# Input stage of a hybrid decoder block: layer norm of the meta tokens and the low-rank rests on other engines, and another order of turned pieces

## The chip, the cores and the metric

The kernel runs on one core of one Trainium2 chip. The metric is the device time of one execution in microseconds (us). Engines: TensorE (PE), VectorE (DVE), ScalarE (ACT), GpSimd (POOL) and SyncE (SP, which here only issues transfers).

## The reference

16 learned meta tokens are put ahead of 256 tokens, all of width 2048, and go through a layer norm, whose output feeds every projection of the block.

```python
def layer_norm(x, g, b):
    mu = jnp.mean(xf, axis=-1, keepdims=True)
    var = jnp.mean(jnp.square(xf - mu), axis=-1, keepdims=True)
    return ((xf - mu) * lax.rsqrt(var + LN_EPS) * g + b).astype(x.dtype)

h = layer_norm(jnp.concatenate([meta, x], axis=1), ln_in_g, ln_in_b)
p = h @ w_in[l]     # r, k, v (2048 columns each), low-rank wl, al, gl (96 + 96 + 256), pool (1024), gates (4096)
...                 # rwkv7 time mixing and causal pooling, merged by gates, output product, layer norm
h = layer_norm(DN_ALPHA * h + peer_ffn(h, ...), ln2_g[l], ln2_b[l])   # 8 x 16 experts per token, gathered rows
return h[:, N_META:]
```

## The kernel before

The program is a row of stages, each a block that all engines enter together and leave together: the input stage (`front_stage`), the time mixing, the merge, the output product, and the routing with the experts, whose rows are gathered from memory. The change is in `front_stage` alone.

**What the stage computes.** The tokens lie as rows: `xm` (16 meta tokens, in the memory of `x_turned1`), and `k.h[:, 0]` and `k.h[:, 1]` (128 tokens each, 2048 wide). Each tile is measured (`measure`: four `bn_stats`, aggregate, plus eps, reciprocal), its deviation is the `Sqrt` of ScalarE (`root`), and `centre` subtracts the mean and scales, in place. TensorE turns the tiles by transposes, 128 columns at a time (`turn`), into three PSUM tiles used in rotation; ScalarE evacuates with gamma and beta as scale and bias into `x_turned`; VectorE splits the result into a rounded part and its rest (`rounded`), which together are hT, the stationary input's partner in every product. Each product is made of three matmuls (high by high, high by rest, rest by high: `product`).

**Pieces.** A piece is four of the sixteen 128-column blocks of one token tile; `PIECES` lists (tile, quarter) in order. The meta tokens are turned apart, as 16 narrow transposes, and evacuated by VectorE.

**Low-rank products.** The 448 low-rank columns of `w_in` come in four quarters of the contraction. ScalarE rounds a quarter (`round_lora`, 128 x 1792), VectorE makes its rest (`rest_lora`), and TensorE runs the products of a quarter for four column tiles (`project`, 12 matmuls each) once `quarter_ready(g)` has seen 1 + 2 (g + 1) increments of `s_hT` and g + 1 of `s_wsplit`. Quarter 0 has the turning of pieces 4 to 7 woven into it. Quarters 2 and 3 run column tile by column tile. Then come 48 matmuls of the first half-tiles of r.

**Queues and order.** Every engine runs its list in order, written out by hand:

- SP loads x, the low-rank weights, three w_half, the constants; then it waits for `s_hT` to reach 8 and 9 and loads gamma and beta as wide rows (1 MB each) over `x_turned0` and `x_turned1`; then three more w_half, each behind a `rest_half`.
- ACT: root(0), copy of gamma and beta vectors, root(1), `round_lora(0)`, then the eight pieces, with root(2) ahead of piece 1 and `round_lora` 1 and 2 ahead of pieces (0, 2) and (0, 3), `round_lora(3)`, three `round_half`, and the low-rank outputs.
- DVE: measure meta, measure x0, centre meta, centre x0, measure x1, meta's evacuation, centre x1, split of meta, then `rounded` of the pieces with the four `rest_lora` between them, small vectors, three `rest_half`, and at the end, behind the wide rows, four passes over h (2048 wide) with the four low-rank mixes between them.
- POOL: two memsets and small loads, then nothing.

Of the kernel before, what the change touches and what calls it, by code (L numbers as in the profile page):

```python
# [9 lines left out]
ALU = mybir.AluOpType  # L10
# [3 lines left out]
P = 128  # L14
D = 2048
# [185 lines left out]
def front_stage(k, w):  # L201

    nc = k.nc
    with ExitStack() as ctx:
# [5 lines left out]
        stats, mv, rs = sb("ln_stats", [P, 3, 4, 6]), sb("ln_mean_var", [P, 3, 2]), sb("ln_rstd", [P, 3, 2])  # L210
# [13 lines left out]
        tiles = [(xm, META), (k.h[:, 0, :], P), (k.h[:, 1, :], P)]  # L224
        ORDER4 = (2, 3, 0, 1)
        PIECES = ((0, 0), (0, 1), (1, 0), (1, 1), (0, 2), (1, 2), (0, 3), (1, 3))
        QK, HK = KT // 4, KT // 2
        block = ctx.enter_context(nc.Block())

# [17 lines left out]
        @block.gpsimd  # L247
        def _(pool):
            mu = w["mu_shift"][0, 0:3 * D].rearrange("(r c) -> r c", c=P)
            nc.gpsimd.memset(raw[:], 0.0).then_inc(s_zero, 1)  # L250
            nc.gpsimd.memset(k.mu_lora[:], 0.0).then_inc(s_zero, 1)
            pool.wait_ge(s_zero, 2)
            rows = [mu] + [w[n][0].rearrange("(r c) -> r c", c=P) for n in ("w0", "a0", "k_k", "k_a")]
            rows += [w["r_k"][0].rearrange("(r two) c -> r (two c)", two=2)]
            rows += [w[n][0].rearrange("(r c) -> r c", c=P) for n in ("gn_g", "gn_b")]
            rows += [w["b_gate"][0].rearrange("b (r c) -> (b r) c", c=P), w["pool_scale"][0].rearrange("(r c) -> r c", c=P)]
            at = 0
            for r in rows:
                done = 0
                while done < r.shape[0]:  # L260
                    n = min(r.shape[0] - done, P - at % P)
                    pool.dma_start(raw[at % P:at % P + n, at // P, :], r[done:done + n, :]).then_inc(s_raw, 16)
                    done, at = done + n, at + n
            for i, (c0, n) in enumerate(k.lora_tiles):
                pool.dma_start(k.mu_lora[0:n, i:i + 1], w["mu_shift"][0, c0:c0 + n].rearrange("(n a) -> n a", a=1)).then_inc(s_raw, 16)

        n_dma = 10 + len(k.lora_tiles)

        @block.tensor
        def _(pe):  # L270
# [3 lines left out]
            pe.wait_ge(s_h, 1)  # L274
            for kt in range(KT):
                mm = nc.tensor.transpose(tp[0][:, kt * META:(kt + 1) * META], xm[:, kt * P:(kt + 1) * P], ident[0:META, 0:META])
            mm.then_inc(s_turn, 1)
            def turn(n):
                t, q = PIECES[n]
                pe.wait_ge(s_h, t + 2)  # L280
                if n == 2:
                    pe.wait_ge(s_meta_ev, 1)
                if n > 2:
                    pe.wait_ge(s_ev, n - 2)
                for j in range(4):
                    mm = nc.tensor.transpose(tp[(n + 1) % 3][:, j * P:(j + 1) * P], k.h[:, t, (4 * q + j) * P:(4 * q + j + 1) * P], ident)
                mm.then_inc(s_turn, 1)

            for n in range(4):
                turn(n)  # L290
            pe.wait_ge(s_raw, 16 * n_dma)
            pe.wait_ge(s_gb, 1)
            nc.tensor.transpose(pv[:, 0:P], raw[:, 0, :], ident)
            nc.tensor.transpose(pv[:, P:2 * P], raw[:, 1, :], ident).then_inc(s_pv, 1)

            def project(i, g):
                c0, n = k.lora_tiles[i]
                for kt in range(QK * g, QK * g + QK):
                    mm = product(nc, pp[i][0:n, :], [x[:, kt, c0 - LORA0:c0 - LORA0 + n] for x in (lhigh, lrest)],
                                 (k.hT_high[:, kt, :], k.hT[:, kt, :]), kt == 0, kt == KT - 1)  # L300
                return mm
# [12 lines left out]
            for i in ORDER4:
                for g in range(2, 4):
                    if i == ORDER4[0]:
                        quarter_ready(g)
                    mm = project(i, g)
                mm.then_inc(s_mm, 1)
            for kt in range(KT):  # L320
                g, kh = divmod(kt, HK)
                if kh == 0:
                    pe.wait_ge(k.s_split, g + 1)
                mm = product(nc, k.project[0][:, 0:T], (k.w_high[g][:, kh, :], k.w_rest[g][:, kh, :]),
                             (k.hT_high[:, kt, :], k.hT[:, kt, :]), kt == 0, kt == KT - 1)
                if kh == HK - 1:
                    mm.then_inc(k.s_used, 1)

        @block.scalar
        def _(act):  # L330
# [5 lines left out]
            def root(i):  # L336
                n = tiles[i][1]
                act.wait_ge(s_var, i + 1)
                nc.scalar.activation(rs[0:n, i, 1:2], rs[0:n, i, 0:1], ACT.Sqrt).then_inc(s_rstd, 1)

            root(0)
            act.wait_ge(s_gb_turn, 1)
            nc.scalar.copy(gb[:], pv[:, 256:256 + 2 * KT]).then_inc(s_gb, 1)
            def round_lora(g):
                act.wait_ge(s_w[g], 16)
                nc.scalar.copy(lhigh[:, QK * g:QK * g + QK, :].bitcast(F32R), lraw[:, QK * g:QK * g + QK, :]).then_inc(s_wround, 1)

            root(1)
            act.wait_ge(s_gb, 1)
            round_lora(0)  # L350
            for n, (t, q) in enumerate(PIECES):
                if n == 1:
                    root(2)
                if (t, q) in ((0, 2), (0, 3)):
                    round_lora(q - 1)
                act.wait_ge(s_turn, n + 2)
# [31 lines left out]
        def _(dve):  # L388
            v, d = nc.vector, nc.vector.drain

            def measure(i):
                x, n = tiles[i]
                for j in range(4):
                    v.bn_stats(stats[0:n, i, j, :], x[:, 512 * j:512 * (j + 1)])
                d()
                v.bn_aggr(mv[0:n, i, :], stats[0:n, i, :, :])
                d()
                v.tensor_scalar(rs[0:n, i, 0:1], mv[0:n, i, 1:2], LN_EPS, None, ALU.add)
                d()
                v.reciprocal(rs[0:n, i, 0:1], rs[0:n, i, 0:1]).then_inc(s_var, 1)  # L400

            def centre(i):
                x, n = tiles[i]
                dve.wait_ge(s_rstd, i + 1)
                v.tensor_scalar(x, x, mv[0:n, i, 0:1], rs[0:n, i, 1:2], ALU.subtract, ALU.mult).then_inc(s_h, 1)

            def rounded(n):
                t, q = PIECES[n]
# [6 lines left out]
            dve.wait_ge(s_meta, 16)  # L415
# [18 lines left out]
            def rest_lora(g):  # L434
                dve.wait_ge(s_wround, g + 1)
                rest_bits(v, lrest[:, QK * g:QK * g + QK, :], lraw[:, QK * g:QK * g + QK, :], lhigh[:, QK * g:QK * g + QK, :]).then_inc(s_wsplit, 1)
# [12 lines left out]
            rest_lora(3)  # L449
            dve.wait_ge(s_pv, 1)  # L450
            v.tensor_copy(k.vec[:, 0:8, :], pv[:, 0:P].rearrange("p (v r) -> p v r", r=16))
            v.tensor_copy(k.vec[:, 8:NRAW, :], pv[:, P:P + 64].rearrange("p (v r) -> p v r", r=16))
# [18 lines left out]
                v.tensor_tensor(k.h[:, t, :], k.h[:, t, :], g, op)  # L471

            dve.wait_ge(s_wide, 32)
            dve.wait_ge(s_turn, 1 + 4 * TT)
            residual(gam, ALU.mult, 0)
            mix(0)
            residual(gam, ALU.mult, 1)
# [1506 lines left out]
```

## Time and profile before

| | us |
|---|---|
| median of 3 runs | 2472.67 (2469.45 to 2474.23) |
| span of the profiled execution, its own time | 2469.5 |
| input stage, up to the first matmul of the next stage | 58.9 |
| TensorE / VectorE / ScalarE busy in the first 58.9 us | 40.61 / 45.44 / 27.05 |
| GpSimd busy in the same | 7.88 |
| TensorE / VectorE busy in the span | 2193.7 / 1533.5 |

The profile is of one execution. Lines Lnnn are those of the kernel's file. Matmuls are pipelined, so the shown duration of one is longer than the spacing between two. A helper's line (L182, `rest_bits`, and L197, `product`) stands for all its callers; the tiles' names tell them apart.

### The profile page before, as it was taken

The page shows a single profiled execution, that of the slowest core. Times are in us where ns is not written, and L with a number is a line of the kernel's source. Part 1 is how long each engine was busy: PE and PEld are TensorE (multiplying, and loading weights), DVE is VectorE, ACT ScalarE, POOL GpSimd, SP SyncE. Part 2 cuts the span into 40 slices and gives each one's busy share as a digit, 9 for nine tenths or more (in the row PEclk, how much of TensorE's full clock was granted, in tenths as well). Part 3 has the DMA queues.
Part 4 walks back from the last instruction along what each step waited for, and adds up shares of the span by engine and source line. Part 5 has one row for each costly group of instructions (what it writes and reads, how often), then busy time and mean ns, then how long its engine had stood idle before and what let it go on. Part 6 is the DMA issues. An engine that isn't in the chain of part 4 may idle for free.

```text
span 2469.5 us, 39419 instructions
## 1 busy us (share of the span) xinstructions
PE 2193.7 (89%) x16183; PEld 1536.9 (62%) x16183; DVE 1533.5 (62%) x2579; ACT 727.0 (29%) x1383; POOL 664.8 (27%) x541
## 2 busy tenths in 40 slices
PE   7999999999999999999989888988787787777776
PEld 6899999999989999988644444533332232222222
DVE  7777777787764554456855776677445544444445
ACT  4555555555434444342211111111111000000000
POOL 1000000000000000002555545555545445444442
PEclk9999999999999999999999999999999999999999
DMA  5433333333347666484999999999999999999997
GB/s 198 137 94 86 100 88 89 97 90 86 97 120 224 184 187 182 139 303 181 404 420 423 423 426 427 427 427 428 427 427 427 426 427 427 427 427 427 427 427 290
DMA packets 346278, 708.29 MB, mean 287 GB/s; under 512 B 13834, under 2 KB 270434, under 8 KB 279778
## 3 DMA queue, kind: packets, MB, share of 16 engines
q0 software_dynamic: 74176, 537.01, 51.7%
q1 hardware_dynamic: 271684, 168.55, 23.3%
q8 instruction: 129, 2.11, 0.3%
q14 instruction: 49, 0.40, 0.0%
q10 hardware_dynamic: 240, 0.22, 0.0%
HBM read 703.63 MB, written 2.10 MB: 286 GB/s over the span
## 4 chain that ended last, share of the span: by engine, by line
DMA 33%; PE 15%; DVE 2%; issue 2%; POOL 1%; DVEq 0%; ACT 0%; POOLq 0%; ACTq 0%
DMA down_rows<-in_v_table,experts 25%; PE bank L1695 11%; DMA up_rows<-in_u_table,experts 8%; PE bank L1611 2%; POOL down_rows L1599 1%; DVE up_rows L1811 0%; PE bank L1638 0%; PE bank L1653 0%; PE bank L1659 0%; ACT diagonal L1755 0%; DVE one_hot L1251 0%; DVE expert_sides L1257 0%; PE bank L1621 0%; PE bank L1665 0%; DVE side_index L1230 0%
## 5 line engine op out<-in xcount | busy, mean ns | idle before, releaser
L1695 PE MATMUL bank<-down_rows,diagonal 128*128 128x512 f32 x2032 | 947.7, 611 | 210.7 <-DMA down_rows<-in_v_table,experts 173.1
L1811 DVE CUSTOM_DVE_ANT_0 up_rows<-up_rows,h 128x2048 f32<-128x2048 f32 x256 | 585.2, 2292 | 523.2 <-DMA up_rows<-in_u_table,experts 523.2
L1695 PEld LDWEIGHTS bank<-down_rows,diagonal 128*128 128x128 f32 x2032 | 375.2, 193 | 741.9 <-issue 385.7
L1593 POOL DMA_INDIRECT up_rows<-in_u_table,experts x256 | 286.0, 1117 | 1207.2 <-POOLq L1269 1091.4
L1599 POOL DMA_INDIRECT down_rows<-in_v_table,experts x256 | 370.3, 1446 | 523.5 <-PE bank L1695 510.5
L182 DVE TENSOR_TENSOR w_half_rest<-w_half,w_half_high 128x1024 fp32r<-128x1024 f32 x224 | 273.0, 1221 | 180.8 <-ACT w_half_high L161 178.9
L197 PE MATMUL project<-hT_high,w_half_high 128*128 128x272 f32 (+1 forms) x1152 | 353.5, 307 | 1.6 <-DVE r L909 1.3
L197 PE MATMUL project<-hT_high,w_half_rest 128*128 128x272 f32 (+1 forms) x1152 | 330.6, 287 | 0.0
L197 PE MATMUL project<-hT,w_half_high 128*128 128x272 f32 (+1 forms) x1152 | 330.0, 287 | 0.0
L161 ACT CAST w_half_high<-w_half 128x1024 fp32r<-128x1024 f32 x224 | 234.7, 1051 | 191.3 <-PE merge_ps L197 122.0
L197 PEld LDWEIGHTS project<-hT_high,w_half_high 128*128 128x128 f32 x1152 | 216.9, 188 | 11.3 <-DVE r L909 1.5
L1774 ACT ACTIVATE dots<-dots 128x4 f32<-128x4 f32 x64 | 13.3, 207 | 713.9 <-DVE dots L1811 713.9
L197 PEld LDWEIGHTS project<-hT,w_half_high 128*128 128x128 f32 x1152 | 217.0, 188 | 2.4
L197 PEld LDWEIGHTS project<-hT_high,w_half_rest 128*128 128x128 f32 x1152 | 216.9, 188 | 0.0
L1755 ACT ACTIVATE diagonal<-constants_kept,weights 128x128 f32<-128x128 f32 x256 | 82.3, 394 | 280.0 <-DVE weights L1818 280.0
L1611 PE MATMUL bank<-h1T,query_w 128*128 128x256 f32 x256 | 65.1, 388 | 10.2 <-ACT queryT L1720 10.2
L197 PE MATMUL merge_ps<-yaT_high,w_half_high 128*128 128x256 f32 x256 | 72.7, 284 | 1.4 <-PEq L514 1.4
L1611 PEld LDWEIGHTS bank<-h1T,query_w 128*128 128x128 f32 x256 | 49.5, 194 | 38.2 <-issue 33.8
L197 PE MATMUL merge_ps<-yaT_high,w_half_rest 128*128 128x256 f32 x256 | 72.4, 283 | 0.0
L197 PE MATMUL merge_ps<-yaT_rest,w_half_high 128*128 128x256 f32 x256 | 72.4, 283 | 0.0
L197 PE MATMUL merge_ps<-hT,w_half_high 128*128 128x256 f32 x256 | 72.1, 282 | 0.0
L197 PE MATMUL merge_ps<-hT_high,w_half_rest 128*128 128x256 f32 x256 | 72.0, 281 | 0.0
(338 smaller groups left out, 3013.2 us busy)
## 6 DMA issues: line engine op xcount, KB each, us to landing
w_half<-in_w_in SPq DMA_DIRECT2D x176, 512.0 KB, 4.0
w_half<-in_w_branch_a SPq DMA_DIRECT2D x32, 512.0 KB, 3.9
out_w<-in_w_out SPq DMA_DIRECT2D x16, 1024.0 KB, 5.3
query_w<-in_w_q_peer SPq DMA_DIRECT2D x10, 1024.0 KB, 19.7
w_half<-in_w_branch_b SPq DMA_DIRECT2D x16, 512.0 KB, 3.8
out_w<-in_w_q_peer SPq DMA_DIRECT2D x6, 1024.0 KB, 29.5
up_rows<-in_u_table,experts POOLq DMA_INDIRECT x256, 21.1
down_rows<-in_v_table,experts POOLq DMA_INDIRECT x256, 20.5
```

Of the source, the lines that this page charges most:

```text
L161: self.nc.scalar.copy(self.w_high[g % 3][:].bitcast(F32R), self.w_raw[g % 3][:]).then_inc(self.s_rounded, 1)
L182: return eng.tensor_tensor(low.bitcast(F32R), x, high, ALU.subtract)
L197: mm = nc.tensor.matmul(out, a.bitcast(F32R), b.bitcast(F32R), start=start and n == 0, stop=stop and n == 2)
L1593: pool.indirect_dma_start(ur[n % RU][:], None, w["u_table"][0], bass.IndirectOffsetOnAxis(ap=k.idx[:, t, h, j:j + 1], axis=0)).then_inc(s_ ...
L1599: pool.indirect_dma_start(vr[n % RV][:], None, w["v_table"][0], bass.IndirectOffsetOnAxis(ap=k.idx[:, t, h, j:j + 1], axis=0)).then_inc(s_ ...
L1611: mm = nc.tensor.matmul(pq[i][:, 0:SEQ], k.query_part(h, i, kt), k.h1T[:, kt, :], start=(kt == 0), stop=(kt == KT - 1))
L1695: mm = nc.tensor.matmul(acc[t][c][:], dg[n % RD][:], vr[n % RV][:, quarter(c)], start=(n == 0), stop=(n == last(t, c)), skip_group_check=True)
L1755: nc.scalar.activation(dg[n % RD][:], ident, ACT.Copy, scale=weights[:, n:n + 1]).then_inc(s_diag, 1)
L1774: nc.scalar.activation(x, x, ACT.Gelu).then_inc(s_gelu, 1)
L1811: v.tensor_tensor_reduce(ur[n % RU][:], ur[n % RU][:], k.h[:, n // (HEADS * TOPK), :], 1.0, 0.0, ALU.mult, ALU.add, dots[:, n:n + 1]).then ...
```

## The change

- Meta's sums move to ScalarE: a `Copy` and a `Square` with an accumulated output, and a small step for minus the mean. VectorE only adds eps and takes the reciprocal of 16 values, ScalarE takes the root, GpSimd centres.
- The four rests of the low-rank weights move from VectorE to GpSimd.
- `PIECES` alternates between the token tiles from the first on. TensorE turns piece 0 before the meta tokens, then pieces 1 and 2; piece 3 now comes behind the first 12 low-rank matmuls.
- Each token tile is centred in two instructions, the first 512 columns and the other 1536. For the second tile these lie on either side of the splits of pieces 0 and 1 and of meta.

```diff
-        PIECES = ((0, 0), (0, 1), (1, 0), (1, 1), (0, 2), (1, 2), (0, 3), (1, 3))
+        PIECES = ((0, 0), (1, 0), (0, 1), (1, 1), (0, 2), (1, 2), (0, 3), (1, 3))
+        scrap, sums = turned[0][0:META].rearrange("p k t -> p (k t)"), sb("meta_sums", [META, 4])
@@ gpsimd
+            pool.wait_ge(s_meta_dev, 1)
+            nc.gpsimd.tensor_scalar(xm, xm, minus_mean, deviation, ALU.add, ALU.mult).then_inc(s_meta_h, 1)
+            for g in range(4):
+                pool.wait_ge(s_wround, g + 1)
+                own = slice(QK * g, QK * g + QK)
+                rest_bits(nc.gpsimd, lrest[:, own, :], lraw[:, own, :], lhigh[:, own, :]).then_inc(s_wsplit, 1)
@@ tensor
-                pe.wait_ge(s_h, t + 2)
+                pe.wait_ge(s_h, t * 2 + (1 if q == 0 else 2))
...
-            for n in range(4):
-                turn(n)
+            turn(0)
+            turn_meta()
+            turn(1)
+            turn(2)
...
+                    if g == 0 and n == 0:
+                        turn(3)
@@ scalar
-            root(0)
+            def meta_sums():
+                act.wait_ge(s_meta, 16)
+                nc.scalar.activation(scrap, xm, ACT.Copy, accum_out=total).then_inc(s_meta_sum, 1)
+                act.wait_ge(s_meta_sum, 1)
+                nc.scalar.activation(minus_mean, total, ACT.Copy, scale=-1.0 / D).then_inc(s_meta_sum, 1)
+                act.wait_ge(s_meta_sum, 2)
+                nc.scalar.activation(scrap, xm, ACT.Square, bias=minus_mean, accum_out=squares).then_inc(s_meta_sq, 1)
+            meta_sums()
+            act.wait_ge(s_meta_var, 1)
+            nc.scalar.activation(deviation, squares, ACT.Sqrt).then_inc(s_meta_dev, 1)
             act.wait_ge(s_gb_turn, 1)
             nc.scalar.copy(gb[:], pv[:, 256:256 + 2 * KT]).then_inc(s_gb, 1)
...
-            root(1)
+            root(0)
             act.wait_ge(s_gb, 1)
             round_lora(0)
             for n, (t, q) in enumerate(PIECES):
                 if n == 1:
-                    root(2)
+                    root(1)
@@ vector
+            FIRST, OTHERS = slice(0, 512), slice(512, D)
             measure(0)
-            dve.wait_ge(s_x[0], 16)
-            measure(1)
-            centre(0)
-            centre(1)
-            dve.wait_ge(s_x[1], 16)
-            measure(2)
-            dve.wait_ge(s_gb, 1)
-            dve.wait_ge(s_turn, 1)
+            dve.wait_ge(s_meta_sq, 1)
+            v.tensor_scalar(squares, squares, 1.0 / D, LN_EPS, ALU.mult, ALU.add)
+            d()
+            v.reciprocal(squares, squares).then_inc(s_meta_var, 1)
+            centre(0, FIRST)
+            centre(0, OTHERS)
+            measure(1)
+            dve.wait_ge(s_meta_turn, 1)
...
-            centre(2)
-            d()
+            centre(1, FIRST)
+            rounded(0)
             v.tensor_copy(k.hT_high[:, :, 0:META].bitcast(F32R), meta_turned[:])
...
-            rounded(0)
-            rest_lora(0)
-            rounded(2)
             rounded(1)
-            rounded(3)
-            rest_lora(1)
-            rounded(4)
-            rounded(5)
-            rest_lora(2)
-            rounded(6)
-            rounded(7)
-            rest_lora(3)
+            centre(1, OTHERS)
+            for n in range(2, len(PIECES)):
+                rounded(n)
```

## Rows read from the trace of the kernel before

**Rows 1.** Top of the page.
```profile
span 2469.5 us, 39419 instructions
```

**Rows 2.** Timeline of PE, 0 to 62 us: start, duration, what [idle before it].
```profile
24.43 0.60 PE L197 MATMUL lora_project<-hT_high,lora_weights_high 128*128 128x272 f32 x1 [2.63 <-DVE hT L182]
...
28.45 0.43 PE L197 MATMUL lora_project<-hT_high,lora_weights_rest 128*128 128x272 f32 x1
28.68 0.38 PE L197 MATMUL lora_project<-hT_high,lora_weights_high 128*128 128x272 f32 x1
...
34.19 0.37 PE L197 MATMUL lora_project<-hT_high,lora_weights_high 128*128 128x272 f32 x1
...
40.30 0.29 PE L197 MATMUL lora_project<-hT_high,lora_weights_high 128*128 128x272 f32 x1
...
58.90 0.36 PE L197 MATMUL project<-hT_high,w_half_high 128*128 128x272 f32 x1 [0.33 <-PEq L204]
```

**Rows 3.** Timeline of DVE, 0 to 60 us.
```profile
8.29 2.44 DVE L394 BATCH_NORM_STATS2 ln_stats<-h 128x6 f32<-128x512 f32 x4
...
11.37 0.16 DVE L400 RECIPROCAL ln_rstd<-ln_rstd 128x1 f32<-128x1 f32 x1
...
12.69 1.33 DVE L405 TENSOR_SCALAR h<-h,ln_mean_var,ln_rstd 128x2048 f32<-128x2048 f32 x1
...
17.66 0.42 DVE L428 TENSOR_TENSOR meta_turned<-meta_turned,ln_in_vectors 128x256 f32<-128x256 f32 x1
...
37.73 0.42 DVE L411 CAST hT_high<-x_turned 128x512 fp32r<-128x512 f32 x1
38.23 0.69 DVE L182 TENSOR_TENSOR hT<-x_turned,hT_high 128x512 fp32r<-128x512 f32 x1
39.09 2.03 DVE L182 TENSOR_TENSOR lora_weights_rest<-lora_weights,lora_weights_high 128x1792 fp32r<-128x1792 f32 x1 [0.16 <-ACT lora_weights_high L346]
...
46.80 2.29 DVE L471 TENSOR_TENSOR h<-h,x_turned 128x2048 f32<-128x2048 f32 x1 [1.28 <-DMA x_turned<-in_ln_in_b]
...
57.02 0.49 DVE L467 SCALAR_TENSOR_TENSOR lora<-lora_project,mu_lora,lora 96x271 f32<-96x271 f32 x1
```

**Rows 4.** DMA issues in 0 to 64 us: size, time to landing.
```profile
x_turned<-in_ln_in_b SPq DMA_DIRECT2D x1, 1024.0 KB, 7.8
```

**Rows 5.** DMA issues in 0 to 0.9 us.
```profile
h<-in_x SPq DMA_DIRECT2D x1, 1024.0 KB, 6.2
```

**Rows 6.** Timeline of ACT, 0 to 60 us.
```profile
11.67 0.21 ACT L339 ACTIVATE ln_rstd<-ln_rstd 128x1 f32<-128x1 f32 x1
12.96 1.69 ACT L346 CAST lora_weights_high<-lora_weights 128x1792 fp32r<-128x1792 f32 x1 [1.08 <-DMA lora_weights<-in_w_in]
...
31.55 1.52 ACT L359 ACTIVATE x_turned<-project,ln_in_vectors 128x128 f32<-128x128 f32 x4
32.93 1.72 ACT L346 CAST lora_weights_high<-lora_weights 128x1792 fp32r<-128x1792 f32 x1
34.52 1.55 ACT L359 ACTIVATE x_turned<-project,ln_in_vectors 128x128 f32<-128x128 f32 x4
```

**Rows 7.** Groups by form, POOL.
```profile
L250 POOL MEMSET raw_vectors<- 128x256 f32 x1 | 0.3, 312 | 0.3 <-POOLq L1976 0.3
...
L251 POOL MEMSET mu_lora<- 128x4 f32 x1 | 0.1, 102 | 0.0
```

**Rows 8.** Timeline of POOL, 1155 to 1260 us, expert stage.
```profile
1231.15 1.91 POOL L1593 DMA_INDIRECT up_rows<-in_u_table,experts  x1 [0.31 <-issue]
1233.37 2.77 POOL L1599 DMA_INDIRECT down_rows<-in_v_table,experts  x1 [0.30 <-issue]
1236.44 0.94 POOL L1593 DMA_INDIRECT up_rows<-in_u_table,experts  x1 [0.30 <-issue]
```

**Rows 9.** Timeline of DVE, same stretch.
```profile
1232.65 0.41 DVE L1807 TENSOR_SCALAR gates<-gates,gate_rsum 128x16 f32<-128x16 f32 x1
1233.03 2.29 DVE L1811 CUSTOM_DVE_ANT_0 up_rows<-up_rows,h 128x2048 f32<-128x2048 f32 x1
```

More of the change, by code:

```diff
@@ L209, in front_stage @@
         raw, gb_raw, gb = sb("raw_vectors", [P, 2, P]), sb("ln_in_rows", [2 * KT, P]), sb("ln_in_vectors", [P, 2 * KT])
-        stats, mv, rs = sb("ln_stats", [P, 3, 4, 6]), sb("ln_mean_var", [P, 3, 2]), sb("ln_rstd", [P, 3, 2])
+        stats, mv, rs = sb("ln_stats", [P, TT, 4, 6]), sb("ln_mean_var", [P, TT, 2]), sb("ln_rstd", [P, TT, 2])
         xm = turned[1][0:META].rearrange("p k t -> p (k t)")
@@ L223, in front_stage @@
         ident = k.kept[:, C_ID:C_ID + P]
-        tiles = [(xm, META), (k.h[:, 0, :], P), (k.h[:, 1, :], P)]
         ORDER4 = (2, 3, 0, 1)
-        PIECES = ((0, 0), (0, 1), (1, 0), (1, 1), (0, 2), (1, 2), (0, 3), (1, 3))
+        PIECES = ((0, 0), (1, 0), (0, 1), (1, 1), (0, 2), (1, 2), (0, 3), (1, 3))
+        scrap, sums = turned[0][0:META].rearrange("p k t -> p (k t)"), sb("meta_sums", [META, 4])
+        total, minus_mean, squares, deviation = (sums[:, i:i + 1] for i in range(4))
+        s_meta_sum, s_meta_sq, s_meta_var, s_meta_dev, s_meta_h, s_meta_turn = (k.sem(f"in_meta_{n}") for n in ("sum", "squares", "var", "deviation", "h", "turned"))
         QK, HK = KT // 4, KT // 2
@@ L273, in _, with turn_meta @@
             nc.tensor.transpose(pv[:, 256:256 + 2 * KT], gb_raw[:], ident[0:2 * KT, 0:2 * KT]).then_inc(s_gb_turn, 1)
[L274 to L277, printed above, removed]
+            def turn_meta():
+                pe.wait_ge(s_meta_h, 1)
+                for kt in range(KT):
+                    mm = nc.tensor.transpose(tp[0][:, kt * META:(kt + 1) * META], xm[:, kt * P:(kt + 1) * P], ident[0:META, 0:META])
+                mm.then_inc(s_meta_turn, 1)
             def turn(n):
                 t, q = PIECES[n]
-                pe.wait_ge(s_h, t + 2)
+                pe.wait_ge(s_h, t * 2 + (1 if q == 0 else 2))
                 if n == 2:
@@ L334, in _, with root @@
                 act.dma_start(gb_raw[n * KT:(n + 1) * KT, :], w[g].rearrange("(r c) -> r c", c=P)).then_inc(s_gb_raw, 16)
[L336 to L339, printed above, removed]
-            root(0)
+            def root(t):
+                act.wait_ge(s_var, t + 1)
+                nc.scalar.activation(rs[:, t, 1:2], rs[:, t, 0:1], ACT.Sqrt).then_inc(s_rstd, 1)
+            def meta_sums():
[8 more added lines that the diff above has]
+            nc.scalar.activation(deviation, squares, ACT.Sqrt).then_inc(s_meta_dev, 1)
             act.wait_ge(s_gb_turn, 1)
@@ L352, in _ @@
                 if n == 1:
-                    root(2)
+                    root(1)
                 if (t, q) in ((0, 2), (0, 3)):
                     round_lora(q - 1)
-                act.wait_ge(s_turn, n + 2)
+                act.wait_ge(s_turn, n + 1)
                 for j in range(4):
@@ L389, in _, with measure, centre @@
             v, d = nc.vector, nc.vector.drain
-            def measure(i):
-                x, n = tiles[i]
+            def measure(t):
+                dve.wait_ge(s_x[t], 16)
                 for j in range(4):
-                    v.bn_stats(stats[0:n, i, j, :], x[:, 512 * j:512 * (j + 1)])
+                    v.bn_stats(stats[:, t, j, :], k.h[:, t, 512 * j:512 * (j + 1)])
                 d()
-                v.bn_aggr(mv[0:n, i, :], stats[0:n, i, :, :])
+                v.bn_aggr(mv[:, t, :], stats[:, t, :, :])
                 d()
-                v.tensor_scalar(rs[0:n, i, 0:1], mv[0:n, i, 1:2], LN_EPS, None, ALU.add)
+                v.tensor_scalar(rs[:, t, 0:1], mv[:, t, 1:2], LN_EPS, None, ALU.add)
                 d()
[L400 to L405, printed above, removed]
+                v.reciprocal(rs[:, t, 0:1], rs[:, t, 0:1]).then_inc(s_var, 1)
+            def centre(t, own):
+                x = k.h[:, t, own]
+                dve.wait_ge(s_rstd, t + 1)
+                v.tensor_scalar(x, x, mv[:, t, 0:1], rs[:, t, 1:2], ALU.subtract, ALU.mult).then_inc(s_h, 1)
             def rounded(n):
@@ L413, in rounded @@
                 rest_bits(v, k.hT[:, own, at], turned[t][:, own, :], k.hT_high[:, own, at]).then_inc(s_hT, 1)
-            dve.wait_ge(s_meta, 16)
+            FIRST, OTHERS = slice(0, 512), slice(512, D)
             measure(0)
-            dve.wait_ge(s_x[0], 16)
-            measure(1)
-            centre(0)
-            centre(1)
-            dve.wait_ge(s_x[1], 16)
-            measure(2)
-            dve.wait_ge(s_gb, 1)
-            dve.wait_ge(s_turn, 1)
+            dve.wait_ge(s_meta_sq, 1)
[4 more added lines that the diff above has]
+            centre(0, OTHERS)
+            measure(1)
+            dve.wait_ge(s_meta_turn, 1)
             wide = lambda c: gb[:, c * KT:(c + 1) * KT].rearrange("p (k a) -> p k a", a=1).to_broadcast((P, KT, META))
@@ L433, in _ @@
             rest_bits(v, k.hT[:, :, 0:META], meta_turned[:], k.hT_high[:, :, 0:META]).then_inc(s_hT, 1)
-            def rest_lora(g):
-                dve.wait_ge(s_wround, g + 1)
-                rest_bits(v, lrest[:, QK * g:QK * g + QK, :], lraw[:, QK * g:QK * g + QK, :], lhigh[:, QK * g:QK * g + QK, :]).then_inc(s_wsplit, 1)
-            rounded(0)
-            rest_lora(0)
-            rounded(2)
-            rounded(1)
-            rounded(3)
-            rest_lora(1)
-            rounded(4)
-            rounded(5)
-            rest_lora(2)
-            rounded(6)
-            rounded(7)
-            rest_lora(3)
+            rounded(1)
+            centre(1, OTHERS)
+            for n in range(2, len(PIECES)):
+                rounded(n)
             dve.wait_ge(s_pv, 1)
@@ L473, in _ @@
             dve.wait_ge(s_wide, 32)
-            dve.wait_ge(s_turn, 1 + 4 * TT)
+            dve.wait_ge(s_turn, 4 * TT)
             residual(gam, ALU.mult, 0)
```

## The prediction

> **What bounds the kernel now.** I read the page first for the span, 2469.5 us [rows 1]; the launch adds nothing to it that the times show, since the shown runs' median is 2472.67 and their lowest 2469.45. The sum below is made against the 2469.5 of the profiled execution and its difference is then added to 2472.67. The change lies wholly in the input stage, so I read the timelines of that stage, engine by engine. TensorE is the one that sets its end: it starts the low-rank products at 24.43, released by a hT from VectorE, and runs without a hole to 58.57, since the first matmul of the next stage stands at 58.90 with 0.33 of idle ahead of it [rows 2]. Inside lie three gates: quarter 1 begins at 34.19, quarter 2 at 40.30, quarter 3 twelve matmuls later, 40.30 + 12 x 0.125 = 41.8, and 16.8 us follow that. Early matmuls come 0.23 us apart (28.45 to 28.68), later ones (6.1 us for the 48 of quarter 1) about 0.127. The engine had idled 2.63 before 24.43, and the spacing halves 4.2 us after it; that is the step from its 1.2 to its 2.4 GHz level [rows 2].
>
> VectorE is close behind. It waits until 46.80 for the second wide row (ln_in_b), then needs 10.7 us for four multiplications and additions of h and the four mixes, and ends at 57.51 [rows 3], only 1.06 before TensorE. That transfer is issued when the ninth hT is counted, at 38.23 + 0.69 = 38.92 [rows 3], and lands 7.8 us later [rows 4]. So the stage has two ends: TensorE's products, and ninth hT + 18.6 us.
>
> **The change part by part.** *Meta off VectorE.* Measuring a tile takes 11.53 - 8.29 = 3.24 there, and centring it 1.33 (rows of x; the same lengths hold for 16 partitions) [rows 3]. The second instruction group started at 8.29, so the meta tokens were there at about 5.1; x's first tile is there at 0.75 + 6.2 = 6.95 [rows 5]. So x0's measure now ends at 10.2, 1.3 earlier. ScalarE's two passes over 2048 elements cost at most 1.72 x 2048 / 1792 = 2.0 each [rows 6], 5.1 to 9.4 with the small one, hidden under x0's measure. VectorE's two small steps end about 10.6, ScalarE's root 10.85.
>
> But root(0) stands behind the copy of the gamma and beta vectors, which put the root of x0 at 11.67 to 11.88 before [rows 6], and nothing there moves. x0 cannot be centred before 11.95.
>
> *Meta's centring on GpSimd.* No row of before shows GpSimd reading an operand and writing a result. Its nearest rows are the memsets: 312 ns for 256 elements, 102 for 4 [rows 7], or 0.83 ns per element for one access. One access for 2048 elements is 1.8 us, two in turn 3.5. I take 2.2, nearer the lower end because the one read and the one write can overlap: 10.9 to 13.1. Three and a half would put the first half-stage 1.3 later at most.
>
> *Low-rank rests on GpSimd.* VectorE does one of 1792 elements in 2.03 [rows 3]; four are removed from it, 8.1 us. GpSimd's floor is the same 2.0; two accesses in turn are 3.1, three (two reads, one write) 4.6. I take 3.8, between the two memset multiples, and keep 2.0 and 4.6. The Trainium skill, GPSIMD Engine Reference, section 3.1, gives 4497 ns for a two-input operation of 2048 elements; as an estimate that is 3.9 for 1792, and the sum would be 0.4 dearer by it. No run here shows it yet.
>
> *Can the two engines work side by side?* In the expert stage a GpSimd gather issue takes 0.94 alone (1236.44), but the one that began at 1233.37 under a two-input VectorE instruction (1233.03 to 1235.32) took 2.77 and ended 0.82 after that one's end; and VectorE's scaling of 16 elements at 1232.65 took 0.41 and ended at 1233.06, the instant at which the GpSimd issue of 1231.15 ended [rows 8, 9]. Each waits for the other, whole instruction by whole instruction. I take this for the rests too, since hT's casts and rests work on the same memory; that they do not wait is the second rival. The Trainium skill, SBUF — State Buffer, section Who interferes with whom, says this as a rule: the pair of ports is locked for a whole instruction, by GpSimd, by VectorE's fast copies and scalings, and for reads by its two-input operations. By that rule the sum is the 5.6 worked out below; without it, the second rival's -1.0. These two rows agree with it.
>
> *The front half with this.* x0's centring waits for GpSimd: first quarter 13.1 to 13.5, the rest to 14.5; x1 measured by 17.8. Rest 0 on GpSimd runs from 14.65, when the first rounding ends [rows 6], to 18.45. Meta's multiply ends at 18.2, its addition (0.42 [rows 3]) has two inputs and waits: 18.45 to 18.85. Centring x1's first quarter to 19.3, four transposes to 20.4, four evacuations (1.4) to 21.85, rounding and rest of the piece (0.42 and 0.69, start to end 1.15 [rows 3]) to 23.1. TensorE starts about 23.15, a gain of 1.3.
>
> *Quarters 0 and 1.* Before, from start to quarter 1 was 9.75. One piece more is now turned inside, four transposes, at the fast spacing at most 4 x 0.127 = 0.5: 10.25, so 33.4. That turn(3) also moves ScalarE: its evacuation comes only after 12 slow matmuls, 23.15 + 2.7 + 0.9, and ends at 28.0. Behind it in ScalarE's order stand rounding 1 (1.6 start to start, evacuations 1.4 [rows 6]): to 29.6, pieces 4 and 5 to 32.4, rounding 2 to 34.0, pieces 6 and 7 to 36.8, rounding 3 to 38.4, only a little ahead of where it ended before (VectorE's last rest, at 39.09, had waited for it [rows 3]). So ScalarE's chain gives nothing back, and rest 1 is 29.6 to 33.4, just in time for 33.4.
>
> *Quarters 2 and 3.* VectorE's rounding of piece 4 is ready at 31.0 but waits for rest 1: 33.4 to 34.6. Rest 2, ready at 34.0, then holds to 38.4. VectorE casts piece 5 to 38.85, rest 3 slips into the gap ahead of its rest and holds to 42.65. Behind it come the rest of piece 5 (43.35), piece 6 (44.5), piece 7 (45.6). TensorE needs piece 5 at 33.4 + 6.1 = 39.5 and gets it at 43.35; quarter 3 opens at 45.6 in place of 41.8, so it ends at 45.6 + 16.8 = 62.4. The ninth hT comes 45.6 - 38.92 = 6.7 late. SP's queue holds the w_half loads behind the wide rows; the next stage needs them only some 4 us into it, and they have that. VectorE ends 57.51 + 6.7 = 64.2, the next stage starts 0.33 later at 64.5: **5.6 us later than 58.90**.
>
> Later stages begin at a barrier behind this one and pass a shift on whole: 2469.5 + 5.6 = 2475.1 for a profile, and 2472.67 + 5.6 = 2478.3 for the median.
>
> With GpSimd's rest at 4.6 the ninth hT falls at 30.4 + 3 x 4.6 + 4.6 = 48.8: +8.8. At 3.1 the turns interleave better and it is 43.25: +3.3. At 2.0 nothing is late and the earlier start remains: -1.0.
>
> **Rivals.** *VectorE keeps the memory between its cast and its rest, or the GpSimd rest costs about 3.1.* Then pieces 4 and 5 go together to 35.7, rest 2 to 39.5, pieces 6 and 7 to 41.8, rest 3 to 45.6. The wide rows are 2.9 late, but TensorE waits for rest 3 at 45.6 and the next stage begins at 62.7: +3.8, median 2476.5; the cheaper rest gives +3.3. For it: nothing in rows 8 and 9 has exactly a cast with its drain. Against it: rest 3 is last in either order, so the sum hardly falls below 3.
>
> *The engines run side by side* (other side: no slower). Then x0 is centred at 11.95, TensorE starts at 21.75, quarter 1 at 32.0, ScalarE's last rounding ends at 37.0, rest 3 at 40.8, where TensorE arrives at 39.6. It ends at 40.8 + 16.8 = 57.6: -1.0, 2471.7. The ninth hT is 2.4 early, so VectorE does not decide. With a rest of 3.1 it is -1.7. It decides from a rest under 4.8 on, and needs that rows 8 and 9 mean something of the gather alone. Against it stand both their directions.
>
> *Dearer.* The stall of nearly 4 us before quarter 2 is longer than the 2.63 behind which TensorE ran at its lower level: a second such stretch costs 4.2 / 2 = 2.1, TensorE ends at 64.5 and the next stage begins at 64.8, 0.3 more. Also the w_half loads are released only 2.2 us after the last wide row instead of 4.3, and can slow its landing by up to 2. Together +7.9: 2480.6.
>
> *A gain that can be measured* would need 4.9 us. Even the earliest start and a free rest give 2.
>
> **How the numbers follow.** Within 0.2%, 4.9 us, is about what a measurement of this kernel cannot tell from no change. The likeliest, GpSimd in the gaps with 3.6 to 4.6 per rest, gets 0.45 (+5 to +8.8, 2477.7 to 2481.5 for itself); the smaller loss of 3.3 to 3.8, 0.36; side by side 0.11; the dearer one 0.05; a gain of over 4.9 by something not seen, 0.03. So slower 0.45 + 0.05 = 0.50, same 0.36 + 0.11 = 0.47, faster 0.03. The time is that of the likeliest, 2478.3. The range goes from 2471.5 (side by side) to 2482 (a rest of 4.6 and some loss of landing).
>
> **What the profile after would show.** Right: first low-rank matmul near 23.2; GpSimd rests of 3.8; hT casts of pieces 4 to 6 starting at the end of a GpSimd rest, or stretched; TensorE idle before quarter 2 or 3; wide rows issued near 45; next stage at 64.5. Wrong: hT casts of 0.42 in the midst of a GpSimd rest (side by side), or rests near 2 us, or the wide row landing before 48. The forecast fails most easily by who gets the memory first, and by the length of one GpSimd rest, each 0.1 us of which counts 0.4.

## The result, and the profile after

The changed kernel takes 2477.57 us (median of 13 runs, 2475.35 to 2479.27) against 2471.95 for the one before (13 runs): ratio 1.0027, 95% interval 1.002 to 1.0034, so 0.27% or 6.6 us slower (the two medians by themselves lie 5.6 apart). The forecast was 2478.3, 5.6 more than before.

The page of the profiled execution has the span:

```profile
span 2476.0 us, 39420 instructions
```

That is 6.5 more than [rows 1]. TensorE's timeline (start, duration, what, idle before it) shows where it comes from:

```profile
23.53 0.59 PE L197 MATMUL lora_project<-hT_high,lora_weights_high 128*128 128x272 f32 x1 [1.54 <-DVE hT L182]
...
34.85 0.36 PE L197 MATMUL lora_project<-hT_high,lora_weights_high 128*128 128x272 f32 x1 [0.76 <-POOL lora_weights_rest L182]
...
44.62 0.40 PE L197 MATMUL lora_project<-hT_high,lora_weights_high 128*128 128x272 f32 x1 [3.50 <-DVE hT L182]
...
65.40 0.36 PE L197 MATMUL project<-hT_high,w_half_high 128*128 128x272 f32 x1 [0.89 <-PEq L204]
```

The next stage begins at 65.40 where it was 58.90 [rows 2]: 6.50 later, as much as the whole difference of the two spans. TensorE starts its products 0.9 earlier, waits 0.76 for GpSimd's rest 1 before quarter 1 and 3.50 for VectorE's hT before quarter 2, and has no hole after that. GpSimd's timeline:

```profile
11.15 2.04 POOL L269 TENSOR_SCALAR x_turned<-x_turned,meta_sums 16x2048 f32<-16x2048 f32 x1 [2.50 <-ACT meta_sums L364]
14.82 3.97 POOL L182 TENSOR_TENSOR lora_weights_rest<-lora_weights,lora_weights_high 128x1792 fp32r<-128x1792 f32 x1 [1.63 <-ACT lora_weights_high L369]
30.66 4.04 POOL L182 TENSOR_TENSOR lora_weights_rest<-lora_weights,lora_weights_high 128x1792 fp32r<-128x1792 f32 x1 [11.87 <-ACT lora_weights_high L369]
35.04 4.07 POOL L182 TENSOR_TENSOR lora_weights_rest<-lora_weights,lora_weights_high 128x1792 fp32r<-128x1792 f32 x1 [0.33 <-ACT lora_weights_high L369]
39.42 4.09 POOL L182 TENSOR_TENSOR lora_weights_rest<-lora_weights,lora_weights_high 128x1792 fp32r<-128x1792 f32 x1 [0.32 <-ACT lora_weights_high L369]
```

A rest takes 3.97 to 4.09, twice VectorE's 2.03 [rows 3]. VectorE's timeline beside it:

```profile
11.92 2.54 DVE L428 TENSOR_SCALAR h<-h,ln_mean_var,ln_rstd 128x512 f32<-128x512 f32 x2 [1.34 <-ACT ln_rstd L352]
...
18.06 1.02 DVE L451 TENSOR_TENSOR meta_turned<-meta_turned,ln_in_vectors 128x256 f32<-128x256 f32 x1
...
32.02 2.96 DVE L434 CAST hT_high<-x_turned 128x512 fp32r<-128x512 f32 x1 [1.79 <-ACT x_turned L382]
35.06 4.59 DVE L182 TENSOR_TENSOR hT<-x_turned,hT_high 128x512 fp32r<-128x512 f32 x1
39.58 4.22 DVE L434 CAST hT_high<-x_turned 128x512 fp32r<-128x512 f32 x1
...
46.07 0.69 DVE L182 TENSOR_TENSOR hT<-x_turned,hT_high 128x512 fp32r<-128x512 f32 x1
...
54.36 2.29 DVE L482 TENSOR_TENSOR h<-h,x_turned 128x2048 f32<-128x2048 f32 x1 [3.19 <-DMA x_turned<-in_ln_in_b]
...
64.58 0.49 DVE L478 SCALAR_TENSOR_TENSOR lora<-lora_project,mu_lora,lora 96x271 f32<-96x271 f32 x1
```

Read the two together. The cast of piece 4 (0.42 before) begins at 32.02 inside rest 1, lasts 2.96 and ends 0.28 after it. The rest of the same piece (0.69 before) is issued at 35.06, 0.02 after rest 2, lasts 4.59 and ends 0.54 after it. The cast of piece 5 is issued at 39.58, inside rest 3, and lasts 4.22. These three have become 11.77 us where they were 1.53. The last rest of a piece, the ninth hT, ends at 46.76, where [rows 3] have 38.92. The second wide row lands at 54.36, and VectorE ends at 65.07, 7.56 later than before. Its transfer was no dearer (time to landing, 7.8 in [rows 4]):

```profile
x_turned<-in_ln_in_b SPq DMA_DIRECT2D x1, 1024.0 KB, 7.5
```

ScalarE's timeline: the rounding for rest 1 begins at 28.89, because piece 3 is turned inside the products, and rounding 3 ends at 39.34, nearly where it ended before. The table load at 9.55 is new; the root of meta waits for it.

```profile
9.55 1.28 ACT L364 ACT_TABLE_LOAD   x1
10.84 0.20 ACT L364 ACTIVATE meta_sums<-meta_sums 16x1 f32<-16x1 f32 x1
...
28.89 1.70 ACT L369 CAST lora_weights_high<-lora_weights 128x1792 fp32r<-128x1792 f32 x1
...
37.54 1.80 ACT L369 CAST lora_weights_high<-lora_weights 128x1792 fp32r<-128x1792 f32 x1
```

The window after the hole shows what else it cost. Its columns are the length of the window, the busy time of TensorE, its weight loads, VectorE, ScalarE and GpSimd (with instructions in brackets), then the granted TensorE clock (PEclk), the DMA share and GB/s:

```profile
45.00:49.00 4.00, 4.00 (x22) 4.00 (x21) 3.83 (x13) 0.00 (x0) 0.00 (x0) 0.57 0.63 221
```

Between 45 and 49 the granted clock is 0.57, mostly its lower level of 1.2 GHz, after 3.50 idle; these 4 us hold 22 matmuls, and the same window of the kernel before holds 34. From 49 on the clock reads 1.00 again.

### The profile page after: what moved, and what is told of

The parts are those of the page before. It is cut to its first block, busy times and chain, and to the rows that moved or that the text cites. A ratio compares the mean times of both kernels' runs of the same rounds, so it can differ in the third digit from the quotient of the medians.

```text
span 2476.0 us, 39420 instructions
## 1 busy us (share of the span) xinstructions
PE 2194.6 (89%) x16183; PEld 1537.8 (62%) x16183; DVE 1533.4 (62%) x2571; ACT 730.7 (30%) x1389; POOL 682.6 (28%) x546
## 4 chain that ended last, share of the span: by engine, by line
DMA 33%; PE 15%; DVE 2%; issue 2%; POOL 1%; DVEq 1%; ACT 0%; POOLq 0%; ACTq 0%
DMA down_rows<-in_v_table,experts 25%; PE bank L1706 12%; DMA up_rows<-in_u_table,experts 8%; PE bank L1622 2%; POOL down_rows L1610 1%; DVE up_rows L1822 0%; PE bank L1649 0%; PE bank L1664 0%; PE bank L1670 0%; ACT diagonal L1766 0%; DVE one_hot L1262 0%; PE bank L1638 0%; DVE expert_sides L1268 0%; PE bank L1632 0%; PE bank L1676 0%
```

## The experiments

Theory: GpSimd's rests and VectorE's casts and rests exclude each other for whole instructions, and this delays hT. Rivals: the new order of pieces costs the time; or GpSimd's rests are merely slow and TensorE waits for them.

**All four rests back on VectorE**, the rest of the change kept.

```diff
-            for g in range(4):      # gpsimd
-                pool.wait_ge(s_wround, g + 1)
-                ...
+            rest_lora(0)            # vector, ahead of rounded(1)
             rounded(1)
             centre(1, OTHERS)
+            ...                     # rest_lora(1), (2), (3) behind pieces 3, 5, 7
```

> The changed kernel with the four low-rank rests back on VectorE (rest 0 ahead of piece 1, the others as before); all else of the change stays. Theory (GpSimd and VectorE exclude each other instruction by instruction, and that makes hT and so the wide rows late): no cast or rest of VectorE longer than 0.7 us (rests 2.03), TensorE starts its low-rank products about 24.5 (rest 0 stands ahead), no hole before quarter 2, ninth hT about 39.7, next stage about 59.4, whole kernel 0 to +1 us against the one before. Rival (the new order of pieces and the turning of piece 3 inside the products cost the time): ninth hT still past 44, next stage still about 65.

Measured: ratio 0.9998 (0.999 to 1.0007). Timelines of TensorE and of VectorE:

```profile
23.62 0.60 PE L197 MATMUL lora_project<-hT_high,lora_weights_high 128*128 128x272 f32 x1 [2.45 <-DVE hT L182]
...
41.35 0.36 PE L197 MATMUL lora_project<-hT_high,lora_weights_high 128*128 128x272 f32 x1 [0.31 <-DVE lora_weights_rest L182]
...
58.51 0.36 PE L197 MATMUL project<-hT_high,w_half_high 128*128 128x272 f32 x1 [0.33 <-PEq L204]
```

```profile
32.83 0.69 DVE L182 TENSOR_TENSOR hT<-x_turned,hT_high 128x512 fp32r<-128x512 f32 x1
...
38.33 0.69 DVE L182 TENSOR_TENSOR hT<-x_turned,hT_high 128x512 fp32r<-128x512 f32 x1
```

No VectorE instruction of pieces 2 to 7 is stretched, the ninth hT is at 39.02, the next stage at 58.51. TensorE waits 0.31 for rest 3, which I had not expected. The rest of the change, the order of pieces, the moved meta sums and the centring in two parts, is thus worth together nothing that can be measured; in the changed kernel the whole 6.5 us go away with the rests' new place. The next stage comes 0.9 earlier than I had expected.

TensorE starts 0.81 earlier than before, and it is not meta's doing. VectorE's centring of the second token tile, in the kernel before and then in this one:

```profile
18.00 1.34 DVE L405 TENSOR_SCALAR h<-h,ln_mean_var,ln_rstd 128x2048 f32<-128x2048 f32 x1
```

```profile
18.18 0.54 DVE L424 TENSOR_SCALAR h<-h,ln_mean_var,ln_rstd 128x512 f32<-128x512 f32 x1
```

It begins 0.18 later here, although VectorE no longer measures or centres meta. What was won ahead of it went in the wait for the root of x0 (1.13 of idle before 11.47) and for GpSimd's centring of meta (10.93 to 12.97, beside which the two centrings of x0 took 2.76). The gain is the second tile's, centred in two parts: the splits begin 0.46 after the start of its centring (18.64), where they began 1.44 after it (19.44). That is 0.98 less, or 0.80 with the 0.18.

**Only the rests moved**, on the kernel before.

```diff
+            for g in range(4):      # gpsimd, behind its small loads
+                pool.wait_ge(s_wround, g + 1)
+                rest_bits(nc.gpsimd, lrest[:, own, :], lraw[:, own, :], lhigh[:, own, :]).then_inc(s_wsplit, 1)
-            rest_lora(0)            # vector, and (1), (2), (3)
```

> The kernel before with nothing but the four rests moved to GpSimd. Theory: rests of 4.0 us, VectorE's casts and rests of pieces 4 to 7 stretched by up to 4 us, ninth hT about 44.4 to 45.5 instead of 38.92, next stage 4.4 to 5.5 later than 58.90, whole kernel +4 to +6 us. Rival (GpSimd is only slower, 4.0 for 2.03, and hides behind nothing else): the last rest ends 2 later than before, about 42.7, VectorE's pieces come no later than before, next stage about 59.8, whole kernel +1.

Measured: ratio 1.0009 (1.0001 to 1.0018), +2.2 us with an interval of 0.2 to 4.4, where I had expected 4 to 6. Timelines:

```profile
44.04 0.39 PE L197 MATMUL lora_project<-hT_high,lora_weights_high 128*128 128x272 f32 x1 [2.87 <-DVE hT L182]
...
62.76 0.36 PE L197 MATMUL project<-hT_high,w_half_high 128*128 128x272 f32 x1 [0.33 <-PEq L204]
```

```profile
35.28 2.98 DVE L415 CAST hT_high<-x_turned 128x512 fp32r<-128x512 f32 x1 [1.79 <-ACT x_turned L363]
38.75 4.14 DVE L182 TENSOR_TENSOR hT<-x_turned,hT_high 128x512 fp32r<-128x512 f32 x1 [0.49 <-issue]
...
43.30 0.69 DVE L182 TENSOR_TENSOR hT<-x_turned,hT_high 128x512 fp32r<-128x512 f32 x1
```

A cast of 2.98 and a rest of 4.14: two held instructions, where the changed kernel has three. Ninth hT 43.99, next stage 62.76, 3.9 later; both a little less than expected. The interval of the time does not exclude the rival's +1, the held instructions and the stage in the profile do. Here rest 1 ran early (25.96) and pieces 4 and 5 were through before rest 2 began; in the changed kernel piece 3 is turned inside the products, and rest 1 begins only at 30.66, just ahead of piece 4. So the same move costs 3.9 in the order before and 6.5 in the new one: the remaining 2.6 come from the two together, since the new order alone cost nothing. (This profile's span, 2471.8, is only 2.3 longer than before, and that of the next experiment 1.7 longer with 4.8 in the stage: the later stages of two executions differ by some us of themselves.)

**Each GpSimd rest in four instructions** of 448 columns, on the changed kernel.

```diff
-                rest_bits(nc.gpsimd, lrest[:, own, :], lraw[:, own, :], lhigh[:, own, :]).then_inc(s_wsplit, 1)
+                for j in range(QK * g, QK * g + QK):
+                    ins = rest_bits(nc.gpsimd, lrest[:, j, :], lraw[:, j, :], lhigh[:, j, :])
+                ins.then_inc(s_wsplit, 1)
```

> The changed kernel with each GpSimd rest cut into 4 instructions of 448 columns, so that VectorE can get in between. Theory (the hold lasts one instruction): each VectorE cast or rest waits at most about 1.1 us, ninth hT about 41 to 42 instead of 46.8, but the last GpSimd rest ends about 46 to 47, so TensorE decides: next stage about 63 to 64, 1 to 2 us earlier than the changed kernel. Rival (no hold; a long GpSimd instruction only slows both alike): ninth hT not earlier than 46, next stage 65.4 or, with the extra starts, 0.3 to 0.6 later.

Measured: ratio 1.0024 (1.0015 to 1.0033). Timelines:

```profile
46.57 0.37 PE L197 MATMUL lora_project<-hT_high,lora_weights_high 128*128 128x272 f32 x1 [1.51 <-POOL lora_weights_rest L182]
...
63.74 0.36 PE L197 MATMUL project<-hT_high,w_half_high 128*128 128x272 f32 x1 [0.33 <-PEq L204]
```

```profile
34.58 1.35 DVE L435 CAST hT_high<-x_turned 128x512 fp32r<-128x512 f32 x1
...
41.71 1.48 DVE L182 TENSOR_TENSOR hT<-x_turned,hT_high 128x512 fp32r<-128x512 f32 x1
```

The first cast of the eight instructions of pieces 4 to 7 lasts 1.18, the others 1.35 to 1.48: their own 0.42 or 0.69 and a wait of 0.8 to 1.0, less than one GpSimd piece (1.1, from the 4.40 of rest 0's four). The two engines take turns. The hold is one instruction long, as the theory has it. The ninth hT comes at 43.19 (I had said 41 to 42; there are eight such waits in a row), the last GpSimd rest is what TensorE waits for at 46.57, and the next stage starts at 63.74, 1.7 earlier than in the changed kernel. The measured times do not tell the two apart.

**Idle rests.** GpSimd does three quarters of each rest into a tile that nobody reads; the real rests are VectorE's. (A tile for whole rests has no room in SBUF: its allocation left 224 bytes a partition where the next tensor needs 512.)

```diff
+                own = slice(QK * g, QK * g + 3)
+                wait(pool, s_idle, g)
+                rest_bits(nc.gpsimd, idle[:], lraw[:, own, :], lhigh[:, own, :]).then_inc(s_idle, 1)
```

> The changed kernel with the four low-rank rests back on VectorE, while GpSimd makes three quarters of each of the same rests (128 x 1344, about 3.0 us), at the moments when the roundings end, into a tile that nobody reads or waits for. Only the neighbourhood of the change is left, no dependency. Theory (exclusion, instruction by instruction): VectorE instructions stretched by up to 3.0 us beside the idle rests 1 to 3, ninth hT 5 to 7 us later than the 39.0 of the kernel with the rests back on VectorE alone, next stage 63 to 65 instead of 58.5. Rival (only the dependency on slow rests cost the time): every VectorE instruction as long as before, next stage 58.5.

Measured: ratio 1.0039 (1.0025 to 1.0053). Timelines of GpSimd, VectorE and TensorE:

```profile
30.93 8.15 POOL L182 TENSOR_TENSOR idle_rest<-lora_weights,lora_weights_high 128x1344 fp32r<-128x1344 f32 x2 [13.05 <-ACT lora_weights_high L371]
39.71 3.14 POOL L182 TENSOR_TENSOR idle_rest<-lora_weights,lora_weights_high 128x1344 fp32r<-128x1344 f32 x1 [0.63 <-ACT lora_weights_high L371]
```

```profile
32.83 3.30 DVE L436 CAST hT_high<-x_turned 128x512 fp32r<-128x512 f32 x1
36.20 3.43 DVE L182 TENSOR_TENSOR hT<-x_turned,hT_high 128x512 fp32r<-128x512 f32 x1
...
40.04 3.36 DVE L182 TENSOR_TENSOR hT<-x_turned,hT_high 128x512 fp32r<-128x512 f32 x1
```

```profile
45.49 0.57 PE L197 MATMUL lora_project<-hT_high,lora_weights_high 128*128 128x272 f32 x1 [5.47 <-DVE lora_weights_rest L182]
...
69.15 0.36 PE L197 MATMUL project<-hT_high,w_half_high 128*128 128x272 f32 x1 [0.33 <-PEq L204]
```

No rest and no hT depends on GpSimd's rests here, and yet the stage is longer than the changed kernel's (the intervals of the two times overlap). A cast of 3.30 and rests of 3.43 and 3.36 stand beside idle rests of 3.0 to 3.1. The first row holds two idle rests in 8.15 us: the first of them had to wait for VectorE's low-rank rest, which had begun at 30.89, 0.04 ahead of it, and kept its 2.02. The next stage comes at 69.15, past the 63 to 65 I gave, and the ninth hT at 47.54, 8.5 later than without the idle rests: the low-rank rests, behind the held pieces, became late too, with 5.47 of idle before quarter 2.

**Idle memsets**, three of 128 x 1344 in each place.

```diff
-                rest_bits(nc.gpsimd, idle[:], lraw[:, own, :], lhigh[:, own, :]).then_inc(s_idle, 1)
+                nc.gpsimd.memset(idle[:], 0.0).then_inc(s_idle, 1)
```

> As the run with idle rests, but GpSimd only writes: three memsets of 128 x 1344 (about 1.1 to 1.2 us each) at each of the four moments, into the tile that nobody reads. If what is held is the whole memory path, casts and rests of VectorE are stretched alike, by up to 1.2 us each. If a write-only GpSimd instruction leaves the second reading path free, the two-input rests (0.69, and 2.03 for the low-rank ones) keep their length and only casts (0.42) and centrings are stretched. The Trainium skill, SBUF — State Buffer, section Who interferes with whom, states the second. Next stage by the second about 59 to 60, by the first 60 to 62.

One profile, 2471.98 us. Timelines of GpSimd and VectorE:

```profile
31.12 3.94 POOL L275 MEMSET idle_rest<- 128x1344 f32 x3 [12.49 <-ACT lora_weights_high L371]
35.50 4.05 POOL L275 MEMSET idle_rest<- 128x1344 f32 x3 [0.44 <-ACT lora_weights_high L371]
```

```profile
34.59 0.76 DVE L436 CAST hT_high<-x_turned 128x512 fp32r<-128x512 f32 x1
35.42 0.69 DVE L182 TENSOR_TENSOR hT<-x_turned,hT_high 128x512 fp32r<-128x512 f32 x1
36.03 2.02 DVE L182 TENSOR_TENSOR lora_weights_rest<-lora_weights,lora_weights_high 128x1792 fp32r<-128x1792 f32 x1
```

Inside the memsets from 35.50 to 39.55 VectorE's low-rank rest at 36.03 keeps its 2.02, and the piece's rest at 35.42 its 0.69. The cast at 34.59, under the memsets of 31.12 to 35.06, takes 0.76 for 0.42. The cast at 37.96 keeps its 0.42, and there it is a memset that takes longer, 1.48 for 1.22. Next stage 59.85, as expected. The Trainium skill (SBUF — State Buffer, Who interferes with whom) has it that a two-input operation of VectorE contends with a GpSimd instruction that reads SBUF, not with one that only writes it; the trace agrees.

**Only rest 0 on GpSimd.**

```diff
-            for g in range(4):      # gpsimd
+            for g in range(1):
```

> The changed kernel with rest 0 on GpSimd and rests 1 to 3 back on VectorE. Rest 0 meets only meta's addition there. Theory: TensorE starts its products at 23.5 to 23.6, no VectorE instruction is stretched after 19, next stage 58.4 to 58.6, level with the kernel with all four back. Rival (each GpSimd rest costs its share of the 6.5 us): next stage about 60.

One profile, 2472.12 us, next stage 58.86, a little later than the 58.4 to 58.6 expected but far from the 60 of an equal share for each rest. TensorE starts at 23.66, as in the first experiment (23.62), and no VectorE instruction is stretched after 19.2. The next stage comes 0.35 later than in the first experiment. That is TensorE's spacing: matmuls in the window 27 to 28, this kernel and then the first experiment's (PE count in brackets):

```profile
27.00:28.00 1.00, 1.00 (x6) 1.00 (x5) 0.00 (x0) 0.36 (x2) 0.00 (x0) 1.00 0.00 0
```

```profile
27.00:28.00 1.00, 1.00 (x11) 1.00 (x10) 0.00 (x0) 0.72 (x3) 0.00 (x0) 1.00 0.00 0
```

In the first experiment the engine already ran 11 matmuls a microsecond, here still 6. Taken over the stage its work lasts 34.25 there (34.56 from start to end, less the wait of 0.31 for rest 3) and 34.87 here: the spacing costs 0.6, of which the missing wait gives back 0.3. The granted clock reads 1.00 in both windows, so this difference is told by the spacing alone.

**Wide rows early**, on the changed kernel.

```diff
-        gam, bet = (t[:].rearrange("p k t -> p (k t)") for t in turned)
+        gam, bet = (lraw[:].rearrange("p k c -> p (k c)")[:, n * D:(n + 1) * D] for n in range(2))
-                sp.wait_ge(s_hT, 2 + PIECES.index((n, 3)))
+                sp.wait_ge(s_wsplit, 2 + n)
```

> The changed kernel, but the two wide rows go to the memory of the low-rank weights and are issued when GpSimd's rests 1 and 2 are done, so they no longer hang on the ninth hT. Theory (the stage has two ends): VectorE's tail starts right after its third half-tile rest at 51.1 and ends near 62; TensorE, held before quarter 2 and slow after it, ends at 64.5 as before and now decides alone: next stage 64.8 to 64.9 instead of 65.40. Rival (the late wide rows are the whole loss): next stage about 62.2, or 59.

One profile, 2476.84 us. Timelines of TensorE, VectorE and GpSimd:

```profile
44.25 0.59 PE L197 MATMUL lora_project<-hT_high,lora_weights_high 128*128 128x272 f32 x1 [3.32 <-DVE hT L182]
...
64.42 0.36 PE L197 MATMUL project<-hT_high,w_half_high 128*128 128x272 f32 x1 [0.33 <-PEq L204]
```

```profile
34.89 0.69 DVE L182 TENSOR_TENSOR hT<-x_turned,hT_high 128x512 fp32r<-128x512 f32 x1
35.50 4.30 DVE L434 CAST hT_high<-x_turned 128x512 fp32r<-128x512 f32 x1
...
60.94 0.49 DVE L478 SCALAR_TENSOR_TENSOR lora<-lora_project,mu_lora,lora 96x271 f32<-96x271 f32 x1
```

```profile
34.89 8.75 POOL L182 TENSOR_TENSOR lora_weights_rest<-lora_weights,lora_weights_high 128x1792 fp32r<-128x1792 f32 x2 [0.37 <-ACT lora_weights_high L369]
```

VectorE is done at 61.43 and no longer decides; TensorE ends at 64.09 and the next stage starts at 64.42, earlier than the 64.8 to 64.9 expected. Not all of the 65.40 - 64.42 = 1.0 is the wide rows', since TensorE itself ends 0.4 earlier than the changed kernel's 64.51 (its ninth hT comes at 46.40, not 46.76). In the changed kernel TensorE alone would have let the next stage start at 64.51 + 0.33 = 64.84. So the late wide rows cost 0.6 there, and 5.9 of the 6.5 stand in TensorE's own waits and clock.

This run also shows the other order of turns. VectorE's rest of piece 4 and GpSimd's rest 2 are both issued at 34.89; VectorE goes first and keeps its 0.69, GpSimd waits, and the next cast is held for 4.30. The ninth hT comes almost at the same time.

No version beat both kernels by more than can be measured. The one with all rests back is level with before.

## Why the prediction was right, point by point

- **Exclusion.** Taken from two instants of the expert stage [rows 8, 9]; shown by the idle rests and by the cut rests.
- **Length of a GpSimd rest.** 3.8 taken, 3.97 to 4.09 measured. Each 0.1 was to count 0.4, so 0.7 to 1.2, and the forecast fell short by 6.5 - 5.6 = 0.9; but that the two agree is chance. From the start of rest 1 to the ninth hT I had 45.6 - 29.6 = 16.0, and it took 46.76 - 30.66 = 16.1: the longer rests were made up for, as VectorE's held instructions ended 0.28, 0.54 and 0.29 after the three GpSimd rests, where I had let it finish the whole of piece 4 between two of them. The 0.9 is rest 1's late start (1.1) and the tail behind the ninth hT (18.3 for 18.6).
- **Front half.** TensorE's start: 23.15 said, 23.53 measured. x0's centring did wait for GpSimd (two instructions, 2.54 from 11.92 on, for about 1.4), and meta's addition for rest 0 (1.02 for 0.42). Not foreseen: the second table load, 1.28, behind which meta's root stands at 10.84 instead of 10.65. Nor does the prediction say that meta's move buys nothing: the centring of x1 begins at 19.00 here and at 18.00 before, and TensorE starts earlier because rest 0 (2.02) and most of that centring no longer stand ahead of the second piece's split.
- **Quarter 1.** 33.4 said, 34.85 measured: ScalarE's chain behind piece 3 ran 1.0 later than I had it, so rest 1 began at 30.66 and not 29.6, and the rest itself was longer. 0.4 of this is TensorE's later start; another 0.4 is the way from there to piece 3's evacuation (3.97, not 3.6). The step was right (rest 1 arrives with TensorE), the size 1.4 short.
- **Quarters 2 and 3.** I let VectorE finish piece 4 before rest 2. It did not: GpSimd went first by 0.02 us. The order differs, the sum hardly, since in either case three rests, and most of four pieces, stand in one line; the run with early rows, where VectorE went first at that point, has its ninth hT at 46.40. Quarter 2 at 43.35 said, 44.62 measured; ninth hT at 45.6 and 46.76.
- **Two ends.** VectorE was said to end at 64.2, ended 65.07; the next stage followed at 65.40. The wide row's landing was not slowed by the w_half loads (7.5 against 7.8), so that part of the dearer rival fell. Its sum was also too high: a stage with two ends starts its next by the later one, so 2 more on VectorE's 64.2 would have made 66.5, or +7.6, and not +7.9.
- **Clock.** The other part of the dearer rival came true: 0.57 between 45 and 49. TensorE ended at 64.51. From the ninth hT at 46.76, 16.8 us at the higher level would give 63.6, so the clock cost TensorE 0.9; behind VectorE's 65.07 it was hidden in the changed kernel.
- **Rivals.** Side by side (-1.0) is refuted. So is the smaller loss for the changed kernel; the kernel before with only its rests moved came out near it, at 3.9 in the stage.
- **The time.** That 2477.57 lies so close to 2478.3 is in part luck: the forecast stood on 2472.67 for the kernel before, whose median is now 2471.95, 0.7 lower, and this hid most of the 0.9 by which the step was too small.

## What to carry to other kernels

Before work moves to GpSimd to relieve VectorE, count the holds: in these traces a GpSimd instruction that reads SBUF stops VectorE's SBUF casts, scalings and two-input operations for its whole length, 4.0 us for work that VectorE did in 2.0. It was nearly free where VectorE idled or did what is not held (rest 0 cost 0.6 in all), and shorter instructions shared the delay out but did not remove it. Look also at what hangs on the delayed engine's count: here it released the transfers that the stage's tail waits for. And ask of each part of a change whether the time that it frees is then spent in another wait: meta's sums left VectorE, and the second tile was centred no earlier.

## What the runs showed of the hardware

- Which of the two goes first between two VectorE instructions is not fixed. GpSimd did in the changed kernel (35.04 ahead of 35.06, 39.42 ahead of 39.58), VectorE in the run with early rows (both at 34.89). With many short instructions the two take turns.
- A GpSimd rest that goes first is hardly stretched by the VectorE instructions that wait for it: 3.97 with little beside it, 4.09 with held instructions waiting. One that comes second waits: two rests took 8.75 in the run with early rows, and an idle one 4.92 instead of 3.02 beside VectorE's low-rank rest.
- Not held by a GpSimd rest (rest 0 of the changed kernel, 14.82 to 18.79): the four statistics instructions of x1 (2.46, before 2.45) and a two-input operation with one input in PSUM (0.40, before 0.42). The same operation with both inputs in SBUF, at 18.06, took 1.02 for 0.42.
- A GpSimd memset that goes first holds a VectorE cast (0.76 for 0.42), but leaves a two-input operation at its full speed (2.02 at 36.03).
- TensorE's granted clock was 0.57 between 45 and 49, behind a hole of 3.50, and 0.64 there behind a hole of 2.87 with only the rests moved; with the cut rests, whose hole before 46.57 was 1.51, it read 1.00. After the start of the products the spacing halved before 27.2 in one kernel and at 28.1 in another that had started within 0.04 us of it; why is open, since the granted clock reads 1.00 in both, and it makes 0.6 us of TensorE's time in this stage.
